# Two transformer blocks on one core: GpSimd's low parts, the first rows' products, the compressed scores and the rotations are ordered anew

## The chip, the cores and the metric

The kernel runs on one NeuronCore of a Trainium2 chip. Its engines run side by side, each in the order of its own instructions, and wait for each other by semaphores: TensorE (PE in the profile, its weight loads PEld) multiplies, VectorE (DVE), ScalarE (ACT) and GpSimd (POOL) work elementwise, and SyncE (SP) issues the loads of weights. SBUF is the memory on the chip; PSUM, with 8 banks, takes what TensorE writes. The metric is the time of one execution on the device in microseconds; lower is better.

## The reference, cut to what matters

A sequence of 256 tokens with 1024 features in float32 goes through two different blocks, each of two layers of three sublayers: a feed-forward, a token mixing, a feed-forward.

```python
# first block, per layer l
x = x + 0.5 * swiglu(rms_norm(x, ffn1_norm[l]), ffn1_wg[l], ffn1_wu[l], ffn1_wd[l])
z = rms_norm(x, mix_norm[l]) @ w_in[l]           # rq rk rv rg mq mk mv ca cg
rq, rk = rotary(to_heads(rq), ret_inv), rotary(to_heads(rk), ret_inv)
y_ret = silu(rg) * rms(retention(rq, rk, rv))    # scores * decay, times values
mq, mk = rotary(to_heads(mq), rope_inv), rotary(to_heads(mk), rope_inv)
y_moba = softmax(causal(mq @ mk.T / 8)) @ mv     # 256 tokens are one block
y_conv = conv_module(ca, cg, ...)                # 31 taps over the tokens
x = x + concat([y_ret, y_moba, y_conv]) @ w_out[l]
x = x + 0.5 * swiglu(rms_norm(x, ffn2_norm[l]), ...)
# second block, per layer: the same three steps, each with
n = rms_norm(h, norm_g[l, i]) * (1 + scale) + shift      # from cond @ ada_w
h = h + gate * sublayer(n)     # mixing: NSA with compressed scores, dilated, forgetting
```

## The kernel before

Every float32 product with weights is made of three passes: the weights `raw` are split into a high part `wh` (ScalarE, L2134) and a low part `wl` = raw - wh (VectorE, L2425), the activations into `xh` and `xl` (or `hTh`/`hTl`, `y1h`/`y1l`), and TensorE adds wh·xh, wl·xh and wh·xl (L1819, L1820, L1822). Weights come in units through 4 buffers `raw` and are split in pieces of two blocks of 128 rows ("subs") into 5 buffers each of `wh` and `wl`. Tokens are in two halves, t = 0 and 1, each with its own PSUM bank.

One class, `Order`, writes the order of all engines: its methods call hooks, and each engine's subclass issues its own instructions in them, so the program order of each engine is that of the calls. `take` and `ahead` split three to four pieces ahead of TensorE's use. `fill` first runs every posted function that is due (`post(f, lag)` makes it due `lag` pieces later; LAG is 3), then multiplies one piece of the current job and calls the job's `done`.

**Mixing of the first block** (`mix1`). The jobs are the column groups c, mq, mk, mv, rq, rk, rv, rg. `q_done` (for mq, mk, rq, rk) first gives VectorE three taps of the convolution (`taps(3)`, six instructions on `cacc`, L2637), then `heads_in`: ScalarE copies the rows into `zt` (L2261) and VectorE rotates them there (L2612 to L2617 over `rt`); a post turns `zt` on TensorE (L1792), and ScalarE copies it out (`Trq`, L2253). Beside the jobs runs `attention` over three groups of two heads: `scores` on TensorE (L1943), row minima on VectorE (L2569), exponentials on ScalarE (L2223), normalization (L2239), turns through banks 6 and 7 (L1792), `values` (L1969, always into bank 7), and then ScalarE's `y1h` (L2244) and VectorE's `y1l` (L2598), which frees bank 7. In a step, `values` stands after the first half's `fill`. Retention follows: `ret_scores` (L2015), `ret_decay` on VectorE (L2681, L2682), `ret_values` (L2024 to L2026, bank 7), which ScalarE empties (L2296), and `turn_wo`, which turns the result (`ym`) through a bank from `next_t`, which gives 6 and 7 in turn by `tbank`.

**Seams between sublayers of the second block** (`skewed`). There are six, at about 995, 1187, 1408, 1602, 1794 and 2015 us. The normalization's row scale (`ms` on VectorE L2465, `rr` on GpSimd L2837) becomes a diagonal matrix `dg` (VectorE, L2509), and TensorE turns and scales the input by it (L1866) for t = 0. `first_hi` multiplies t = 0 with what is there (L1880, L1883, L1887) while the other half is still being added up; then come the second diagonal, the second turn, and `first_lo` and `first_rest`. At all seams but the first, the two low parts that are still open go to GpSimd (`split_lo_pool`, L2831).

**Compressed scores** (`cmp_scores`, L2080, second block). Four heads, two rows of tokens each: 64-row products of 15 columns. Even heads lie in partitions 0 to 63 and write bank 4, odd heads in 64 to 127 and bank 5. Float32 products like these are two passes each in the profile.

Of the kernel before, what the change touches and what calls it, by code (L numbers as in the profile page):

```python
# [406 lines left out]
class Order:  # L407
# [120 lines left out]
    def lower(self, pool=False):  # L528

        j, u, k0, nk, w, last = self.later.pop(0)  # L530
        if pool:
            self.lo_at[j] = (self.s.plo, j)
            self.split_lo_pool(j, u, k0, nk, w)
        else:
            self.lo_at[j] = (self.s.lo, j)
            self.split_lo(j, u, k0, nk, w)
        if last:
            self.load(u + NR, self.lo_at[j], self.lo_at[j - 1] if k0 else None)
# [7 lines left out]
    def split_lo_pool(self, j, u, k0, nk, w):  # L546
        pass
# [263 lines left out]
    def skewed(self, label, banks):  # L811

        nx, add_1 = self.half
        s = nx[-1]
# [3 lines left out]
        two = nx[0] == "final"  # L818
# [16 lines left out]
        while self.later:  # L835
            self.lower(pool=not two)
# [388 lines left out]
    def heads_in(self, b, tk, zi, rot, rs):  # L1225
        z = self.m.zt[zi]
        for t in range(2):
            r = self.new(self.s.act, "zin")
            self.rows_part(z[:, t, 0:384], b[t], 384, tk, rs, t, ACT.Copy, self.zt_free[zi], r)
            self.free[b[t]] = r  # L1230
        if rot is not None:
            cos, sin, half, w = rot
            r = self.rotate(z[:, :, 0:384].rearrange("p t (n f) -> p t n f", f=64), cos, sin, 6, half, [r, w])
        return r

# [18 lines left out]
    def mix1(self, l, nx):  # L1254
# [31 lines left out]
        def q_done(n, zi, rot):  # L1286
            def done(b, tk):
                taps(3)
                r = self.heads_in(b, tk, zi, rot, True)

                def post():
                    rdy[n] = self.heads_out(m.qk[n], zi, r)
                self.post(post)
            return done
# [124 lines left out]
        ret_out(2)  # L1419
        turn_wo(0)  # L1420
# [364 lines left out]
class Tensor(Order):  # L1785
# [86 lines left out]
    def first_hi(self, js, b, x):  # L1872
# [11 lines left out]
        j, hs, nk, w = js[2]  # L1884
        self.wait_ge(self.lo_at[j])
        for n in range(nk):
            e.matmul(o, X[0](4 + n, 0), m.wl[hs][:, n * w:(n + 1) * w], start=False, stop=False)  # L1887
# [185 lines left out]
    def cmp_scores(self, l, qn):  # L2073
        m = self.m
        for h in (0, 2, 1, 3):
            lo, b = 64 * (h % 2), 4 + h % 2
            self.wait_ge((self.s.vec, ("kc", l)), *qn, self.free[b])
            for t in range(2):
# [742 lines left out]
class Pool(Order):  # L2821
# [4 lines left out]
    def split_lo_pool(self, j, u, k0, nk, w):  # L2826
# [3 lines left out]
        self.wait_ge((s.hi, j))  # L2830
# [188 lines left out]
```

## Time and profile before

| | us |
|---|---|
| median of 3 runs | 2216.21 (2215.99 to 2217.55) |
| profiled execution | 2214.64 |
| its span in the profile | 2212.8 |
| TensorE busy | 2188.6 (99%) |
| VectorE busy | 1536.3 (69%) |
| ScalarE busy | 1148.3 (52%) |
| GpSimd busy | 49.5 (2%) |
| chain that ended last | PE 91%, DVE 6%, ACT 1%, DMA 1% |

The granted TensorE clock is full throughout (0.999 in the mean). Busy time of TensorE contains the modelled ends of its pipelined passes, so what counts is from start to start: a pass of 512 columns starts every 0.23 us, one of 384 every 0.17 us. The rows of a timeline give the start in us from the beginning of the span, the time in us, the engine, the line of the code, the operation, what is written and read, the number of merged instructions, and in brackets the idle time before and what ended it.

### The profile page before, as it was taken

To read this page: it belongs to the slowest core of one execution; us is meant where nothing else is said; L and a number is where in the kernel's file an instruction comes from. 1 tells how busy PE (TensorE), PEld (TensorE's weight loads), DVE (VectorE), ACT (ScalarE), POOL (GpSimd) and SP (SyncE) were. 2 spreads that over 40 slices of the span, in tenths; PEclk is the share of its full clock that TensorE was granted. 3 is DMA by queue.
4 is the path that set the end of the run, shared out by engine and by line. 5 is a ranking of instruction groups with operands and counts; after the bars stand their busy time and mean duration, and the time that the engine had idled before them with its cause. 6 is when DMAs were issued, how large, how long until landed. Compare 5 with 4: busy or idle time off the path is not lost.

```text
span 2212.8 us, 27002 instructions
## 1 busy us (share of the span) xinstructions
PE 2188.6 (99%) x10836; PEld 1835.7 (83%) x10836; DVE 1536.3 (69%) x2339; ACT 1148.3 (52%) x1759; POOL 49.5 (2%) x42
## 2 busy tenths in 40 slices
PE   8999999999999999999999999999999999999998
PEld 6888888888888888888888977788888889778887
DVE  5655975557886978868785655788678756557664
ACT  5445654444445654445445655544454456555443
POOL 0000010000000010000001000100000010001000
PEclk9999999999999999999999999999999999999999
DMA  8554455556885557776776444577767864445653
GB/s 294 195 193 152 157 172 174 187 202 229 284 283 160 163 191 266 261 263 221 274 276 190 138 150 152 189 267 276 256 228 278 283 196 140 142 152 176 233 200 124
DMA packets 250641, 462.93 MB, mean 209 GB/s; under 512 B 9798, under 2 KB 55792, under 8 KB 250388
## 3 DMA queue, kind: packets, MB, share of 16 engines
q1 hardware_dynamic: 250276, 461.05, 61.0%
q8 instruction: 85, 1.39, 0.2%
q14 instruction: 40, 0.33, 0.0%
q10 hardware_dynamic: 240, 0.16, 0.0%
HBM read 460.12 MB, written 1.05 MB: 208 GB/s over the span
## 4 chain that ended last, share of the span: by engine, by line
PE 91%; DVE 6%; ACT 1%; DMA 1%; issue 0%; POOL 0%; SPq 0%; POOLq 0%; DVEq 0%; ACTq 0%
PE ps L1819 18%; PE ps L1822 18%; PE ps L1820 18%; PE s L1822 8%; PE s L1819 8%; PE s L1820 8%; PE ps L1792 3%; DVE wl L2425 2%; DVE cacc L2637 1%; PE s L1943 1%; PE ps L1835 1%; PE ps L1833 1%; PE ps L1834 1%; PE ps L1969 1%; DVE gts L2811 1%; PE ps L1866 1%
## 5 line engine op out<-in xcount | busy, mean ns | idle before, releaser
L2425 DVE TENSOR_TENSOR wl<-raw,wh 128x1024 fp32r<-128x1024 f32 (+1 forms) x734 | 853.2, 1179 | 218.2 <-ACT wh L2134 213.9
L2134 ACT ACTIVATE wh<-raw 128x1024 fp32r<-128x1024 f32 (+2 forms) x744 | 750.2, 1027 | 463.8 <-PE ps L1822 254.1
L1819 PE MATMUL ps<-wh,xh 128*128 128x512 f32 (+3 forms) x1632 | 619.9, 380 | 1.7 <-DVE wl L2425 1.7
L1822 PE MATMUL ps<-wh,xl 128*128 128x512 f32 (+3 forms) x1632 | 609.9, 374 | 0.0
L1820 PE MATMUL ps<-wl,xh 128*128 128x512 f32 (+3 forms) x1632 | 609.6, 374 | 0.0
L1819 PEld LDWEIGHTS ps<-wh,xh 128*128 128x128 f32 x1632 | 306.6, 188 | 57.0 <-issue 9.5
L1822 PEld LDWEIGHTS ps<-wh,xl 128*128 128x128 f32 x1632 | 306.5, 188 | 47.0
L1820 PEld LDWEIGHTS ps<-wl,xh 128*128 128x128 f32 x1632 | 306.8, 188 | 44.9
L2433 DVE SCALAR_TENSOR_TENSOR acc<-raw,condT,acc 128x512 f32<-128x512 f32 x252 | 188.6, 748 | 5.1
L1819 PE MATMUL s<-wh,xh 128*128 128x512 f32 x384 | 150.3, 391 | 0.0
L1822 PE MATMUL s<-wh,xl 128*128 128x512 f32 x384 | 149.6, 390 | 0.0
L1820 PE MATMUL s<-wl,xh 128*128 128x512 f32 x384 | 149.5, 389 | 0.0
L1819 PE MATMUL s<-wh,hTh 128*128 128x512 f32 x352 | 138.5, 394 | 0.0
L1822 PE MATMUL s<-wh,hTl 128*128 128x512 f32 x352 | 137.3, 390 | 0.0
L1820 PE MATMUL s<-wl,hTh 128*128 128x512 f32 x352 | 137.1, 390 | 0.0
L2216 ACT ACTIVATE hTh<-ps 128x512 fp32r<-128x512 f32 x88 | 48.3, 596 | 162.3 <-PE ps L1792 162.3
L2561 DVE TENSOR_TENSOR hTl<-ps,hTh 128x512 fp32r<-128x512 f32 x88 | 57.0, 686 | 104.0 <-ACT hTh L2216 103.9
L1819 PE MATMUL ps<-wh,hTh 128*128 128x512 f32 x268 | 104.6, 390 | 0.0
L1822 PE MATMUL ps<-wh,hTl 128*128 128x512 f32 x268 | 104.3, 389 | 0.0
L1820 PE MATMUL ps<-wl,hTh 128*128 128x512 f32 x268 | 104.3, 389 | 0.0
L1822 PEld LDWEIGHTS s<-wh,xl 128*128 128x128 f32 x384 | 72.1, 188 | 15.1
L1819 PEld LDWEIGHTS s<-wh,xh 128*128 128x128 f32 x384 | 72.1, 188 | 14.9
(357 smaller groups left out, 2471.3 us busy)
## 6 DMA issues: line engine op xcount, KB each, us to landing
raw<-in_ffn_w_in SPq DMA_DIRECT2D x80, 1024.0 KB, 5.2
raw<-in_ada_w SPq DMA_DIRECT2D x72, 1024.0 KB, 6.0
raw<-in_ffn_wg SPq DMA_DIRECT2D x40, 1024.0 KB, 5.2
raw<-in_ffn_wu SPq DMA_DIRECT2D x40, 1024.0 KB, 5.2
raw<-in_ffn_wd SPq DMA_DIRECT2D x40, 1024.0 KB, 5.3
raw<-in_ffn_w_out SPq DMA_DIRECT2D x40, 1024.0 KB, 6.4
raw<-in_mix_w_in SPq DMA_DIRECT2D x28, 1024.0 KB, 5.1
raw<-in_w_in SPq DMA_DIRECT2D x28, 768.0 KB, 4.3
```

Of the source, the lines that this page charges most:

```text
L1792: return self.e.transpose(out, src, self.m.ident[0:n, 0:n])
L1819: e.matmul(o, X[0](kk, t), hi, start=kk == 0, stop=False)
L1820: e.matmul(o, X[0](kk, t), lo, start=False, stop=False)
L1822: ins = e.matmul(o, X[1](kk, t), hi, start=False, stop=kk == K - 1)
L1833: e.matmul(o, X[0](kk, t), hi, start=kk == 0, stop=False)
L1834: e.matmul(o, X[0](kk, t), lo, start=False, stop=False)
L1835: ins = e.matmul(o, X[1](kk, t), hi, start=False, stop=kk == K - 1)
L2134: ins = self.e.activation(m.wh[j % NH][:, 0:n], m.raw[u % NR][:, k0 * w:k0 * w + n], ACT.Copy)
L2216: self.then_inc(self.e.activation(m.hTh[:, k:k + 2, :].rearrange("p k s -> p (k s)"), m.ps[b], ACT.Copy), th)
L2425: ins = self.e.tensor_tensor(m.wl[j % NH][:, 0:n], m.raw[u % NR][:, k0 * w:k0 * w + n], hi, ALU.subtract)
L2433: ins = self.e.scalar_tensor_tensor(out=a, in0=m.raw[u % NR][:, k * 512:k * 512 + 512], scalar=m.condT[:, kk:kk + 1], in1=a if kk else m.b ...
L2561: self.then_inc(self.e.tensor_tensor(lo, m.ps[b], hi.bitcast(F32), ALU.subtract), tl)
```

## The change

GpSimd's low parts wait, beside their high part, for the first diagonal (`("dg", s, 0)`). In `first_hi` the two low products of the third piece come before the high products of the fourth. `cmp_scores` goes over the heads inside of the loop over the rows of tokens. `heads_in` is cut in two, and `q_done` of the first block's mixing posts taps and rotation for the next `fill`. `tbank` is set to 7 ahead of `turn_wo(0)`, so that this turn takes bank 6.

```diff
-    def lower(self, pool=False):
+    def lower(self, pool=None):
...
-            self.split_lo_pool(j, u, k0, nk, w)
+            self.split_lo_pool(j, u, k0, nk, w, pool)
...
         while self.later:
-            self.lower(pool=not two)
+            self.lower(pool=None if two else (self.s.vec, ("dg", s, 0)))
...
+    def heads_rows(self, b, tk, zi, rs):
+        z = self.m.zt[zi]
         for t in range(2):
             r = self.new(self.s.act, "zin")
             self.rows_part(z[:, t, 0:384], b[t], 384, tk, rs, t, ACT.Copy, self.zt_free[zi], r)
             self.free[b[t]] = r
         return r
+
+    def heads_turn(self, zi, rot, r):
+        cos, sin, half, w = rot
+        z = self.m.zt[zi][:, :, 0:384].rearrange("p t (n f) -> p t n f", f=64)
+        return self.rotate(z, cos, sin, 6, half, [r, w])
...
             def done(b, tk):
-                taps(3)
-                r = self.heads_in(b, tk, zi, rot, True)
+                r = self.heads_rows(b, tk, zi, True)
+
+                def turn():
+                    taps(3)
+                    self.heads_turn(zi, rot, r)
 
                 def post():
-                    rdy[n] = self.heads_out(m.qk[n], zi, r)
+                    rdy[n] = self.heads_out(m.qk[n], zi, self.rt_free)
+                self.post(turn, 0)
                 self.post(post)
...
         ret_out(2)
+        self.tbank = 7
         turn_wo(0)
...
-        j, hs, nk, w = js[2]
-        self.wait_ge(self.lo_at[j])
-        for n in range(nk):
-            e.matmul(o, X[0](4 + n, 0), m.wl[hs][:, n * w:(n + 1) * w], start=False, stop=False)
+            if i == 2:
+                self.wait_ge(self.lo_at[j])
+                for n in range(nk):
+                    e.matmul(o, X[0](4 + n, 0), m.wl[hs][:, n * w:(n + 1) * w], start=False, stop=False)
...
-        for h in (0, 2, 1, 3):
-            lo, b = 64 * (h % 2), 4 + h % 2
-            self.wait_ge((self.s.vec, ("kc", l)), *qn, self.free[b])
-            for t in range(2):
+        self.wait_ge((self.s.vec, ("kc", l)), *qn, self.free[4], self.free[5])
+        for t in range(2):
+            for h in range(4):
+                lo, b = 64 * (h % 2), 4 + h % 2
...
-        self.wait_ge((s.hi, j))
+        self.wait_ge((s.hi, j), after)
```

VectorE in the first mixing, from the last piece ahead of the rotation of `rq` to the next piece (wl_NN and wh_NN are the five buffers, raw_NN the four, `cacc` the taps, zt_105 the rows of `rq`, `y1l` the first group's low part). Before:

```order
L2425 TENSOR_TENSOR wl_65<-raw_54,wh_60 128x768 [waits s_hi]
L2637 SCALAR_TENSOR_TENSOR cacc<-upad,cols_68,cacc 128x256 [waits s_vec] x6
L2612 TENSOR_TENSOR rt_134<-zt_105,cos_72 128x384 [waits s_act]
L2613 TENSOR_TENSOR rt_135<-zt_105,sin_73 128x384
L2614 TENSOR_TENSOR rt_136<-zt_105,cos_72 128x384
L2615 TENSOR_TENSOR rt_137<-zt_105,sin_73 128x384
L2616 TENSOR_TENSOR zt_105<-rt_134,rt_135 128x2x6x32 [waits s_vec]
L2617 TENSOR_TENSOR zt_105<-rt_136,rt_137 128x2x6x32
L2598 TENSOR_TENSOR y1l<-ps,y1h 128x256 [waits s_act]
L2425 TENSOR_TENSOR wl_66<-raw_54,wh_61 128x768
```

The same place now (the lines of the code are 11 higher):

```order
L2436 TENSOR_TENSOR wl_65<-raw_54,wh_60 128x768 [waits s_hi]
L2609 TENSOR_TENSOR y1l<-ps,y1h 128x256 [waits s_act]
L2648 SCALAR_TENSOR_TENSOR cacc<-upad,cols_68,cacc 128x256 [waits s_vec] x6
L2623 TENSOR_TENSOR rt_134<-zt_105,cos_72 128x384
L2624 TENSOR_TENSOR rt_135<-zt_105,sin_73 128x384
L2625 TENSOR_TENSOR rt_136<-zt_105,cos_72 128x384
L2626 TENSOR_TENSOR rt_137<-zt_105,sin_73 128x384
L2627 TENSOR_TENSOR zt_105<-rt_134,rt_135 128x2x6x32 [waits s_vec]
L2628 TENSOR_TENSOR zt_105<-rt_136,rt_137 128x2x6x32
L2436 TENSOR_TENSOR wl_66<-raw_54,wh_61 128x768
```

`y1l`, which waits for ScalarE, moved from behind six taps and the rotation to ahead of them; the place of `rk` a group later, and both in the second layer, moved in the same way. At `mq` and `mk`, where no group is under way, the rotation moved behind two more taps. ScalarE's and SyncE's orders are the same as before.

TensorE at the second seam, from the third piece's high products to the second turn (`dg` the diagonal, s and ps PSUM banks). Before:

```order
L1880 MATMUL ps<-wh_59,xh 128x512 [waits s_act]
L1880 MATMUL ps<-wh_59,xh 128x512
L1880 MATMUL ps<-wh_60,xh 128x512 [waits s_act]
L1880 MATMUL ps<-wh_60,xh 128x512
L1887 MATMUL ps<-wl_64,xh 128x512 [waits s_plo]
L1887 MATMUL ps<-wl_64,xh 128x512
L1866 MATMUL s<-dg,x 128x128 [waits s_vec]
```

And now:

```order
L1891 MATMUL ps<-wh_59,xh 128x512 [waits s_act]
L1891 MATMUL ps<-wh_59,xh 128x512
L1898 MATMUL ps<-wl_64,xh 128x512 [waits s_plo]
L1898 MATMUL ps<-wl_64,xh 128x512
L1891 MATMUL ps<-wh_60,xh 128x512 [waits s_act]
L1891 MATMUL ps<-wh_60,xh 128x512
L1877 MATMUL s<-dg,x 128x128 [waits s_vec]
```

The two low products moved ahead of the wait for the fourth piece's activations, at all six seams; what stands behind them is still the turn by the second diagonal.

## Rows read from the trace of the kernel before

**Rows 1.** The page, busy time of TensorE: us, share of the span, instructions.
```profile
PE 2188.6 (99%) x10836; PEld 1835.7 (83%) x10836; DVE 1536.3 (69%) x2339; ACT 1148.3 (52%) x1759; POOL 49.5 (2%) x42
```

**Rows 2.** Waits of PE: total us, how many times, the longest.
```profile
PE ps L1866 <- DVE dg L2509: 3.0, 2, 2.7
...
PE ps L1880 <- ACT xh L2200: 1.6, 6, 0.5
...
PE ps L1792 <- ACT ptT L2229: 1.1, 2, 0.5
```

**Rows 3.** Busy us of each engine (instructions), clock, DMA, first block's mixing.
```profile
237.00:273.00 36.00, 35.00 (x220) 31.05 (x219) 35.63 (x94) 25.80 (x65) 0.00 (x0) 1.00 0.49 152
```

**Rows 4.** Timeline of DVE: start, us, line, op, out<-in, count, idle before.
```profile
248.79 2.46 DVE L2637 SCALAR_TENSOR_TENSOR cacc<-upad,cols,cacc 128x256 f32<-128x256 f32 x6
...
254.44 0.95 DVE L2425 TENSOR_TENSOR wl<-raw,wh 128x768 fp32r<-128x768 f32 x1
...
257.76 0.28 DVE L2569 CUSTOM_DVE_ANT_0 pt<-s,cst 128x128 f32<-128x128 f32 x1
```

**Rows 5.** Timeline of ACT in the same stretch.
```profile
251.53 0.37 ACT L2244 ACTIVATE y1h<-ps 128x256 fp32r<-128x256 f32 x1
...
258.08 0.40 ACT L2223 ACTIVATE pt<-pt,small 128x128 f32<-128x128 f32 x1 [2.37 <-DVE small L2569]
...
260.59 0.84 ACT L2253 ACTIVATE Trq<-ps 128x512 f32<-128x512 f32 x2
```

**Rows 6.** Timeline of PE, same stretch and some 14 us on.
```profile
258.18 0.82 PE L1792 MATMUL ps<-cst,zt 128*128 128x128 f32 x6
...
261.49 0.76 PE L1969 MATMUL ps<-ptT,mv 128*64 128x256 f32 x6 [0.38 <-ACT Trq L2253]
...
275.15 0.92 PE L2015 MATMUL s<-Trq,Trk 64*128 64x256 f32 x8
```

**Rows 7.** Timeline of DVE, the next group and the first decay.
```profile
261.71 2.46 DVE L2637 SCALAR_TENSOR_TENSOR cacc<-upad,cols,cacc 128x256 f32<-128x256 f32 x6
...
267.36 0.95 DVE L2425 TENSOR_TENSOR wl<-raw,wh 128x768 fp32r<-128x768 f32 x1
...
273.86 0.42 DVE L2681 TENSOR_TENSOR pt<-s,cst 128x256 f32<-128x256 f32 x1 [0.57 <-PE s L2015]
```

**Rows 8.** Timeline of ACT, the next group's high part.
```profile
264.38 0.38 ACT L2244 ACTIVATE y1h<-ps 128x256 fp32r<-128x256 f32 x1
```

**Rows 9.** Timeline of DVE, first op of the rotation of `mq`.
```profile
220.76 0.26 DVE L2612 TENSOR_TENSOR rt<-zt,cos 128x96 f32<-128x96 f32 x1 [0.56 <-ACT zt L2261]
```

**Rows 10.** Timelines of DVE, POOL and PE at the seam at 1408.
```profile
1408.52 2.35 DVE L2509 TENSOR_SCALAR dg<-cst,rr 128x128 f32<-128x128 f32 x1 [0.66 <-POOL rr L2837]
...
1408.45 4.66 POOL L2831 TENSOR_TENSOR wl<-raw,wh 128x1024 fp32r<-128x1024 f32 x2
...
1411.02 0.68 PE L1866 MATMUL ps<-dg,x 128*128 128x128 f32 x4 [2.74 <-DVE dg L2509]
```

**Rows 11.** Timelines of DVE and PE, second diagonal at the seam at 1602.
```profile
1608.26 0.29 DVE L2509 TENSOR_SCALAR dg<-cst,rr 128x128 f32<-128x128 f32 x1 [0.44 <-POOL rr L2837]
...
1608.71 0.56 PE L1866 MATMUL s<-dg,x 128*128 128x128 f32 x3
```

**Rows 12.** Timelines of POOL and DVE at the seam at 2015.
```profile
2015.45 4.76 POOL L2831 TENSOR_TENSOR wl<-raw,wh 128x1024 fp32r<-128x1024 f32 x2
...
2019.95 0.27 DVE L2465 SCALAR_TENSOR_TENSOR ms<-ssq 128x1 f32<-128x1 f32 x1
```

**Rows 13.** Timeline of PE at the seam between the blocks.
```profile
1000.44 0.73 PE L1880 MATMUL ps<-wh,xh 128*128 128x512 f32 x2 [0.49 <-ACT xh L2200]
```

**Rows 14.** Timeline of PE: compressed scores, then a group's scores.
```profile
1229.56 1.53 PE L2080 MATMUL s<-small,qn 64*128 64x15 f32 x16
...
1242.13 0.93 PE L1943 MATMUL s<-kd,qn 64*128 64x128 f32 x8
```

**Rows 15.** Timeline of PE, turn of the retention's output.
```profile
295.67 0.41 PE L1792 MATMUL ps<-cst,ym 128*128 128x128 f32 x2 [0.57 <-ACT zt L2296]
```

More of the change, by code:

```diff
@@ L544, in split_lo, with split_lo_pool @@
         pass
-    def split_lo_pool(self, j, u, k0, nk, w):
+    def split_lo_pool(self, j, u, k0, nk, w, after):
         pass
@@ L1223, in rotate_part @@
         pass
-    def heads_in(self, b, tk, zi, rot, rs):
+    def heads_rows(self, b, tk, zi, rs):
         z = self.m.zt[zi]
@@ L1230, in heads_in @@
             self.free[b[t]] = r
-        if rot is not None:
-            cos, sin, half, w = rot
-            r = self.rotate(z[:, :, 0:384].rearrange("p t (n f) -> p t n f", f=64), cos, sin, 6, half, [r, w])
-        return r
+        return r
+    def heads_turn(self, zi, rot, r):
+        cos, sin, half, w = rot
+        z = self.m.zt[zi][:, :, 0:384].rearrange("p t (n f) -> p t n f", f=64)
+        return self.rotate(z, cos, sin, 6, half, [r, w])
+    def heads_in(self, b, tk, zi, rot, rs):
+        r = self.heads_rows(b, tk, zi, rs)
+        return r if rot is None else self.heads_turn(zi, rot, r)
     def heads_out(self, dst, zi, after, scale=1.0):
@@ L2824, with split_lo_pool @@
     engine = "POOL"
-    def split_lo_pool(self, j, u, k0, nk, w):
+    def split_lo_pool(self, j, u, k0, nk, w, after):
         m, s = self.m, self.s
```

## The prediction

> **What bounds the kernel now.** I read the page's busy times first: TensorE is busy for 2188.6 us of the 2212.8 us span [rows 1]. So an edit gains only where TensorE stands still or where it streams fewer or better overlapped passes, and it loses wherever it makes TensorE wait. The waits by engine then give what can be won: 3.0 us behind the diagonals, 1.6 us in six places behind the high parts `xh`, and pieces of about 0.5 us in the two mixing sublayers of the first block [rows 2]. Last I read where another engine is about to become the bound. In the stretch in which the first block's mixing scores, turns and rotates, VectorE is busy for 35.63 us of 36.00, with TensorE at 35.00 beside it [rows 3]. There VectorE has no slack, and whatever makes it stand still comes back as a TensorE wait.
>
> **Part 1, the rotations later.** This is the largest term. In the order, the low part of an attention group's values (`y1l`) has moved ahead of six taps and the rotation of `rq`, and after that of `rk`. VectorE runs in order, and `y1l` waits for ScalarE's high part `y1h`. Before the change VectorE ended a `wl` piece at 248.79, ran taps and rotation, and went on with the next `wl` at 254.44, with `y1l` in between and no wait [rows 4]. `y1h` ended at 251.53 + 0.37 = 251.90 [rows 5]; its place on ScalarE and what is ahead of it there are not changed. So VectorE would now reach `y1l` at 248.79 and stand still until 251.93. Behind it is the same work as before, 254.44 - 248.79 = 5.65, so the next `wl` starts at 257.58 instead of 254.44: 3.14 us late, with six taps, the rotation, a `wl` and the next group's row minima queued behind the wait.
>
> Who waits for that: the row minima at 257.76 [rows 4] come at 260.90. ScalarE had waited 2.37 us for them at 258.08, and its copy of the turned `rq`, which frees PSUM bank 7, ends at 260.59 + 0.84 = 261.43 [rows 5]. TensorE's products with the values need that bank and had already waited 0.38 us for it at 261.49 [rows 6]. They move to 264.63. The turns of `rq` at 258.18 [rows 6] still find the rotation ended, about 257.7.
>
> The second time goes the same way. VectorE was free at 261.71, now at 264.85; `y1h` ends at 264.38 + 0.38 = 264.76, shifted by the same 3.14 to 267.90 [rows 7, 8]. VectorE stands still for another 3.05 us, and the `wl` of 267.36 [rows 7] starts at 267.93 + 5.65 = 273.58, 6.22 late. The next op that TensorE needs is the retention decay at 273.86, before which VectorE had been idle for 0.57 us [rows 7]; it is 6.22 - 0.57 = 5.65 late, and so are the scores of the second pair of heads at 275.15, which need the banks that the decays free [rows 6]. Nothing later gives that back, since TensorE is the engine that sets the end. What is gained inside: the rotation of `mq` no longer waits 0.56 us for ScalarE, as two more taps stand ahead of it [rows 9]. It bounds the gain at 0 and 0.56; I take 0.3, since later scores wait for TensorE and not for VectorE. That is **5.3 us lost in each of the two mixing sublayers, 10.6 us**. Its bounds are 0 per sublayer (if the backlog is absorbed, rival 1) and 6.2 (if the 0.57 us are not).
>
> **Part 2, GpSimd behind the first diagonal.** At 1408 GpSimd started its two low parts at 1408.45 and VectorE's diagonal, started at 1408.52, took 2.35 us; TensorE waited 2.74 us and started 0.15 us after its end [rows 10]. At 1608 the same op took 0.29 us [rows 11]. With the wait the diagonal is never held: 2.35 - 0.29 = 2.06 us gained, at this one of five places. The wait has a price. At 2015 GpSimd started at 2015.45 for 4.76 us, and VectorE's sum `ms`, ready at 2019.95, took 0.27 us, until GpSimd was done at 2020.21 [rows 12]. GpSimd would now start after the diagonal, 0.25 us later there, and `ms`, the row scale, the second diagonal and TensorE's second turn follow by as much. At 1408 I take 0.3 and for the other three 0.1 together, since there GpSimd just ends before `ms`. **Sum: 2.06 - 0.3 - 0.25 - 0.1 = 1.4 us gained.** The rows show a diagonal and a sum that end only with GpSimd's op. The Trainium skill, SBUF — State Buffer, section "SBUF: two separate sides", says that the port pair of VectorE and GpSimd is an exclusive lock which whichever engine starts first keeps for the whole instruction. By that rule, the trace agrees with both numbers, 2.35 and 0.27 us; without it the later start would cost nothing and the part would give 2.0 us.
>
> **Part 3, the first rows' products reordered.** Two low products now fill the place where TensorE waits for the last `xh`: at most 0.49 us at 1000.44 [rows 13] and about 0.22 us in each of the five others. In those five it gains nothing. The second diagonal starts at 1608.26 for 0.29 us, and TensorE's second turn starts at 1608.71, which is its end plus the 0.15 us of rows 10 [rows 11]. TensorE would only arrive early and wait there. At 1000.44 the row scale isn't the bound, so I take 0.45, between 0 and 0.49. **0.45 us gained.**
>
> **Part 4, the compressed scores.** Sixteen passes of 15 columns take 1.53 us with each head's two rows of tokens behind each other, while eight passes of 128 and 256 columns, whose heads alternate between the two halves of the array, take 0.93 [rows 14]. If alternation overlaps the short ones in pairs as well, a half, 0.77, is the most that can go; nothing is the least. I take 0.4, since the four long pairs show about 0.2 us a pair, and eight short ones at half that come to 0.8 with a tail of 0.3. Two sublayers: **0.8 us gained.** The Trainium skill, TensorEngine Tiling (Array Packing), section "Theoretical Speedup", gives up to 2 times for a contraction of 64 or less. By that the part would be an estimated 1.5 us instead of 0.8.
>
> **Part 5, the bank of the retention's turn.** TensorE waited 0.57 us at 295.67 for ScalarE to empty bank 7, just written by the last retention values [rows 15]. The turn now takes bank 6. Between 0 and 0.57; I take 0.4, since `y1h` and `y1l` of that turn must be ready half a piece of weights later. Twice: **0.8 us gained.** The other mixing sublayers and feed-forwards get banks 6 and 7 swapped; the first block's two mixings ran alike, so I put that at nothing.
>
> **Sum.** Gains 1.4 + 0.45 + 0.8 + 0.8 = 3.45; loss 10.6; together 7.1 us slower. The profiled execution was 2214.64 us with a span of 2212.8, and the median of three is 2216.21; the sum of changes is put on the median: 2223.3 us (the profiled one would be 2221.8).
>
> **The rivals.** (1) The backlog is absorbed: VectorE catches up before TensorE needs anything, so part 1 costs between 0 and 3.8 us per sublayer. For it: after 273 VectorE has room, and pieces of `wl` are made three to four pieces ahead. Against it: the 2.37 us that ScalarE waited on VectorE and the bank that TensorE waited on already [rows 5, 6]. It gives -3.4 to +4.2 us, 2212.8 to 2220.4. (2) On the other side, faster: `y1h` comes early enough, so `y1l` first only frees bank 7 sooner. TensorE's turns of the next group then lose their waits, 1.1 us in two places that the profile puts on ScalarE's `ptT` [rows 2]; my reading is that they wait for `y1l`, which frees the same bank. It decides at `y1h` ending before 248.8 instead of 251.9, and gives -3.45 - 1.1 - 0.8 (short gaps of the same kind) = -5.4, 2210.8. Against it stands that `y1h` sits behind four normalizations in ScalarE's unchanged order. (3) The wait for the diagonal turns against itself, GpSimd's low part being late for TensorE: its first op ends 2.4 us after its start, with more than a us in hand, so I give it no place of its own. The change does in the order what it says.
>
> **How the numbers follow.** The forecast, 2223.3, has a chance of 0.68 and by itself the range 2220.7 to 2226.5 (part 1 between 4 and 6.2 per sublayer, parts 2 to 5 at their ends). Rival 1 has 0.20, rival 2 has 0.12. About 0.2% of the time, 4.4 us, is what a measurement of this kernel can tell from no change. So slower 0.68, within 0.2% 0.20, faster 0.12. The range is 2213.0 to 2226.5: it holds rival 1 and leaves out rival 2 and a few in a hundred above.
>
> **What would show each step.** Part 1: VectorE idle for about 3 us before `y1l` twice in each first-block mixing, waits of TensorE of 3 us more before the values' products, and 5 us more from the first scores to the first retention values. Part 2: every diagonal at 0.29 us, none behind GpSimd, and second diagonals up to 0.3 us later against the first. Part 3: no wait on `xh`, and a new one on the second diagonal in five places. Part 4: sixteen passes in about 1.1 us. Part 5: no wait of the kind of rows 15. I am wrong if VectorE isn't idle at `y1l`, or if it is and TensorE's row is no later at the first retention values.

## The result, and the profile after

The changed kernel takes 2225.12 us (median of 6 executions, 2223.75 to 2226.77), the kernel before 2217.1 us beside it (median of 6, 2215.99 to 2218.05). The ratio is 1.0038, with a 95% interval of 1.0028 to 1.0048: some 8 us, or 0.4%, slower. The profiled execution of after took 2226.47 us with a span of 2224.4. One execution of the kernel before, at 2921 us, is left out of all ratios and counts.

The waits of TensorE in after (engine, tile and line that waited, what for, us in all, times, longest us). The line numbers of the code are 11 higher than in the kernel before:

```profile
PE ps L1980 <- ACT Trq L2264: 7.1, 2, 3.7
PE ps L1803 <- DVE y1l L2609: 2.4, 1, 2.4
PE s L1877 <- DVE dg L2520: 2.4, 5, 0.7
...
PE ps L1877 <- DVE dg L2520: 1.0, 2, 0.7
```

Against [rows 2] the first two are new and long: the values' products wait 3.7 us for `Trq`, and once, for 2.4 us, some transposes wait for `y1l`. The 3.0 us for `dg` have become 1.0, the six waits on `xh` are gone, and five waits on the second diagonal are new. Now VectorE in the first mixing (start, us, engine, line, operation, in brackets the idle time and who ended it):

```profile
253.23 0.42 DVE L2609 TENSOR_TENSOR y1l<-ps,y1h 128x256 fp32r<-128x256 f32 x1 [3.06 <-ACT y1h L2255]
...
269.22 0.42 DVE L2609 TENSOR_TENSOR y1l<-ps,y1h 128x256 fp32r<-128x256 f32 x1 [2.99 <-ACT y1h L2255]
...
280.72 0.42 DVE L2692 TENSOR_TENSOR pt<-s,cst 128x256 f32<-128x256 f32 x1
```

The two idle stretches before `y1l` are as long as worked out. The decays at 280.72 stood at 273.86 [rows 7] and have no idle time before them. TensorE in the first mixing and then in the second:

```profile
265.93 1.33 PE L1980 MATMUL ps<-ptT,mv 128*64 128x256 f32 x6 [3.66 <-ACT Trq L2264]
...
281.11 0.66 PE L1803 MATMUL ps<-cst,cacc 128*128 128x128 f32 x4
282.01 0.92 PE L2026 MATMUL s<-Trq,Trk 64*128 64x256 f32 x8 [0.24 <-DVE pt L2693]
...
762.52 0.87 PE L1980 MATMUL ps<-ptT,mv 128*64 128x256 f32 x8 [3.42 <-ACT Trq L2264]
...
779.21 0.63 PE L1803 MATMUL ps<-cst,cacc 128*128 128x128 f32 x4 [2.44 <-DVE y1l L2609]
```

The transposes of the convolution's output `cacc` go straight on in the first mixing (281.11) and wait 2.44 us in the second (779.21). The kernel before had no wait in either. Two things were not in the prediction: this wait, and the speed of the passes behind the waits. Busy time of the engines by stretch of after (stretch, its length, then PE, PEld, DVE, ACT, POOL busy with their counts, the granted TensorE clock, DMA share, GB/s):

```profile
266.00:272.00 6.00, 6.00 (x22) 5.29 (x23) 3.01 (x9) 4.27 (x10) 0.00 (x0) 0.50 0.47 150
272.00:284.00 12.00, 11.76 (x81) 10.63 (x81) 11.19 (x26) 6.70 (x12) 0.00 (x0) 1.00 0.52 171
...
780.50:784.20 3.70, 3.70 (x16) 3.59 (x13) 3.40 (x9) 0.91 (x1) 0.00 (x0) 0.54 0.18 50
```

Behind the wait of 3.66 us TensorE was granted 0.50, its level of 1.2 GHz, and made 22 passes in 6 us; afterwards it was back at 1.00, 2.4 GHz. In [rows 3] the clock was 1.00 all through.

**Where the time went.** For each matmul the start after less the start before gives an offset. The table has the change of that offset over each part, for the profiled executions; the columns beside it are kernels of the next section.

| part (us in the trace of before) | forecast | after | part 1 taken back | best version |
| --- | --- | --- | --- | --- |
| start of the program (up to 18) | 0 | +1.7 | +2.0 | +1.4 |
| first mixing (225 to 290) | +5.3 | +5.21 | +0.05 | -0.37 |
| retention's turn (290 to 305) | -0.4 | -0.41 | -0.45 | -0.45 |
| second mixing (725 to 783) | +5.3 | +7.57 | +1.04 | -0.43 |
| retention's turn (783 to 800) | -0.4 | -0.44 | -0.44 | -0.45 |
| `acl` (925 to 950) | 0 | +0.35 | -0.56 | -0.09 |
| first rows' products at 1000 | -0.45 | -0.40 | -0.41 | -0.44 |
| compressed scores, both | -0.8 | -0.94 | -0.94 | -0.94 |
| seam at 1408 | -1.76 | -1.71 | -1.69 | -1.69 |
| four other seams | +0.35 | +0.47 | +0.50 | +0.49 |
| last matmul | +7.1 | +11.5 | -0.8 | -3.1 |

Small drifts between the rows make up the rest. The 11.5 us of the traces are more than the 8 us of the medians, since the two profiled executions stand at opposite ends: 2214.64 us is below the before's median and 2226.47 above the after's. The first row, 1.7 us, goes with no part of the change. Passes of 512 columns started every 0.43 us instead of 0.23 between 12 and 16 us. This came in 7 of the 13 traces of changed kernels; after has it, and the kernel `taps_first` of the next section, which holds all five parts too, has not. How many of the executions behind the medians have it isn't known.

The seam at 1408, where the first diagonal had taken 2.35 us [rows 10], in after: TensorE, then VectorE, then GpSimd.

```profile
1422.18 0.68 PE L1877 MATMUL ps<-dg,x 128*128 128x128 f32 x4 [0.66 <-DVE dg L2520]
...
1428.13 1.13 PE L1877 MATMUL s<-dg,x 128*128 128x128 f32 x8 [0.68 <-DVE dg L2520]
```

```profile
1421.75 0.29 DVE L2520 TENSOR_SCALAR dg<-cst,rr 128x128 f32<-128x128 f32 x1 [0.66 <-POOL rr L2848]
...
1426.36 0.56 DVE L2476 SCALAR_TENSOR_TENSOR ms<-ssq 128x1 f32<-128x1 f32 x1 [0.15 <-ACT junk L2165]
...
1427.69 0.29 DVE L2520 TENSOR_SCALAR dg<-cst,rr 128x128 f32<-128x128 f32 x1 [0.44 <-POOL rr L2848]
```

```profile
1422.18 4.73 POOL L2842 TENSOR_TENSOR wl<-raw,wh 128x1024 fp32r<-128x1024 f32 x2 [0.47 <-DVE dg L2520]
1427.00 0.66 POOL L2848 TENSOR_TENSOR rr<-ms,cst 128x1 f32<-128x1 f32 x1
```

The diagonal takes 0.29 us. The price is as read: `ms` lasts 0.56 us instead of 0.16, until GpSimd's op ends at 1426.91, the row scale `rr` follows at 1427.00, and TensorE's second turn waits 0.68 us for the second diagonal.

The compressed scores, [rows 14] before:

```profile
1243.25 1.07 PE L2091 MATMUL s<-small,qn 64*128 64x15 f32 x16
```

1.07 us for the sixteen passes instead of 1.53.

### The profile page after: what moved, and what is told of

It reads as the page before. It is cut to its first block, busy times and chain, and to the rows that moved or that the text cites. A ratio compares the mean times of both kernels' runs of the same rounds, so it can differ in the third digit from the quotient of the medians.

```text
span 2224.4 us, 27009 instructions
## 1 busy us (share of the span) xinstructions
PE 2194.9 (99%) x10836; PEld 1843.0 (83%) x10836; DVE 1535.7 (69%) x2339; ACT 1148.1 (52%) x1759; POOL 48.6 (2%) x42
## 4 chain that ended last, share of the span: by engine, by line
PE 92%; DVE 5%; ACT 2%; DMA 1%; issue 0%; POOL 0%; ACTq 0%; POOLq 0%; SPq 0%; DVEq 0%
PE ps L1830 19%; PE ps L1833 18%; PE ps L1831 18%; PE s L1830 8%; PE s L1833 8%; PE s L1831 8%; PE ps L1803 4%; PE s L1954 1%; DVE wl L2436 1%; PE ps L1846 1%; PE ps L1844 1%; PE ps L1845 1%; DVE cacc L2648 1%; PE ps L1980 1%; DVE gts L2822 1%; PE ps L1877 1%
```

## The experiments

Twelve kernels, each timed beside the kernel before on the same chip. The main theory: part 1 costs some 5.2 us in each first-block mixing by making VectorE stand still; the swapped banks, which the prediction put at nothing, cost the rest of the second mixing; and the half clock behind TensorE's long waits may or may not add to either. The rivals are named with each run.

### Part 1 taken back

```diff
             def done(b, tk):
-                r = self.heads_rows(b, tk, zi, True)
-                def turn():
-                    taps(3)
-                    self.heads_turn(zi, rot, r)
+                taps(3)
+                r = self.heads_in(b, tk, zi, rot, True)
...
-                self.post(turn, 0)
                 self.post(post)
```

> The changed kernel with part 1 taken back: taps and rotation stand again where they stood before, parts 2 to 5 stay. Theory, by the offsets between the two traces: part 1 is the only part that costs much, 5.6 us in the first mixing and up to 8.1 in the second. Without it no wait of VectorE of 3 us before y1l, no 3.7 us wait of TensorE before the values' products, granted clock 1.0 there. What stays: -1.2 us at the five seams (-1.7 at 1408, +0.1 to +0.3 at the others), -0.4 at 1000, -0.5 at each set of compressed scores, -0.4 twice at the retention's turn, and a cost of about 1.1 in the second mixing, where the swapped banks make the transposes of cacc (before at 766.67) wait for y1l (ended at 767.20 + 0.42). Sum -2.3 us, 2214.8. Rival: the swapped banks cost nothing by themselves, sum -3.4, 2213.7. Rival: the loss is not in part 1 (the other edits or the slow clock cause it), time stays above 2221.

Measured: 2213.45 us, before 2216.02, ratio 0.9983 (0.9974 to 0.9992). Both mixings are back, but the second keeps 1.04 us (table above). The sum of the trace without its first row is -2.8, and the rival that the loss lies elsewhere falls. The time is nearer to the 2213.7 of the rival in which the swap costs nothing than to 2214.8, but the trace shows the 1.04 us and the wait on `y1l`. Waits of TensorE:

```profile
PE s L1873 <- DVE dg L2516: 2.4, 5, 0.7
PE ps L1799 <- DVE y1l L2605: 1.8, 2, 1.0
```

### Part 1 alone

The edit above, the other way, in the kernel before.

> The kernel before with part 1 alone. Theory: VectorE idle for 3.1 us before two y1l in each first-block mixing, 5.3 to 5.6 us lost in each, so +10.6 to +11.2, 2227.7 to 2228.3, and both mixings alike since no bank is swapped; the transposes of cacc do not wait in either. The granted clock falls to half behind the wait of 3.7 us before the values' products, hidden behind VectorE's own lateness. Rival: the second mixing costs 8.1 as in the changed kernel, because the lateness alone makes the transposes of cacc wait, +13.5, 2230.6. Rival (backlog absorbed): under +4.

Measured: 2227.36 us, before 2216.02, ratio 1.0048 (1.0034 to 1.0061), some 11 us. By the trace +5.16 in the first mixing and +5.12 in the second. So without swapped banks the two are alike, and lateness alone does not make the transposes of `cacc` wait for `y1l`. They waited 0.20 us, for `cacc` itself:

```profile
777.26 0.63 PE L1802 MATMUL ps<-cst,cacc 128*128 128x128 f32 x4 [0.20 <-DVE cacc L2647]
```

### The retention's turn in bank 6, alone

```diff
         ret_out(2)
+        self.tbank = 7
         turn_wo(0)
```

> The kernel before with part 5 alone (the retention's turn takes bank 6). Theory: 0.4 us gained at each of the two turns; the banks are swapped from there on, so in the second mixing the transposes of cacc share a bank with the y1l whose subtraction ended at 767.62 and cannot start at 766.67: 1.0 to 1.1 us lost at that place, a wait of TensorE on y1l, none in the first mixing. Sum +0.3, 2217.4. Rival: the swap costs only when VectorE is late, no wait at cacc, sum -0.8, 2216.3.

Measured: 2217.08 us, before 2216.02, ratio 1.0003 (0.9994 to 1.0012). The time can't tell the two apart, the trace can: -0.45 at each turn, +1.03 in the second mixing, and this wait of TensorE, right behind VectorE's `y1l`:

```profile
767.03 0.63 PE L1793 MATMUL ps<-cst,cacc 128*128 128x128 f32 x4 [1.03 <-DVE y1l L2599]
```

```profile
766.46 0.42 DVE L2599 TENSOR_TENSOR y1l<-ps,y1h 128x256 fp32r<-128x256 f32 x1
```

The values always go to bank 7, the turns alternate between 6 and 7. Setting the alternation by hand at one place moved every turn behind it to the other bank, and so the transposes of `cacc` of the second mixing to bank 7, just filled by the values. The part was worth nothing in its first form: two gains of 0.45 against one loss of 1.03.

This trace showed more. Behind the first diagonal at 1408, which is held by GpSimd here as before, TensorE ran at half clock, which the kernel before did not do in its profiled execution; the offset grew by 2.34 us there:

```profile
1410.40:1416.50 6.10, 6.07 (x22) 5.57 (x23) 2.61 (x8) 2.94 (x8) 2.11 (x1) 0.50 0.48 146
```

### The changed kernel with the banks' turn put back

```diff
-        self.tbank = 7
+        tb, self.tbank = self.tbank, 7
         turn_wo(0)
+        self.tbank = 13 - tb
```

> The changed kernel, with the banks' turn put back after the first product of part 5, so that the second mixing has the same banks as the first. Theory: the 2.44 us wait of the cacc transposes at 779.21 and the half-clock stretch behind it go; the second mixing costs 5.6 us like the first, not 8.1; 2.4 to 4.0 us below the changed kernel, 2221.1 to 2222.7. Rival: the wait comes from VectorE's lateness and stays, 2225.1.

Measured: 2223.14 us, ratio 1.0030 (1.0019 to 1.0041). Second mixing +5.12, first +5.19, both turns still -0.43. The 2.44 us wait is gone, and the next scores wait for the decays in its place:

```profile
776.19 0.63 PE L1804 MATMUL ps<-cst,cacc 128*128 128x128 f32 x4 [0.20 <-DVE cacc L2649]
778.12 0.92 PE L2027 MATMUL s<-Trq,Trk 64*128 64x256 f32 x8 [1.30 <-DVE pt L2694]
```

So the swap cost 7.57 - 5.12 = 2.45 us in the changed kernel and 1.03 where VectorE is in time. The wait itself is not the larger share of the 2.45. By the offsets, the changed kernel lost 2.47 us from 763 us of the trace of before to these scores and the kernel with the banks put back 1.57, for it waits at the decays instead: 0.9 us between them. Behind the scores the changed kernel lost another 1.55 us, in the stretch at half clock (780.50 above), and the other one nothing. The transposes wait 2.44 us because `y1l` stands behind the late decays, and the clock falls behind that wait.

### Part 1 for rq alone, and for rk alone

```diff
-            return done
+            return later if n in ("rq",) else now
```

`later` is the new form, `now` the old one; `("rk",)` in the second kernel.

> The kernel before with part 1 for rq alone (mq, mk and rk as before). Theory A (VectorE's lateness alone decides, as in the prediction's sum): one idle stretch of 3.14 us per mixing, less the 0.57 us that VectorE had in hand before the decays: 2.6 us per mixing, +5.2, 2221.2; TensorE's half-clock stretch is hidden. Theory B (the clock decides where VectorE is less late): TensorE still waits 3.7 us before the values' products, runs for some 6 us at half clock behind it, and by that is 6 us late itself at the next turns, as the changed kernel showed at 267 us (7.28 - 1.30 against before); so 5 to 5.4 us per mixing although VectorE's part is only 2.6; +10 to +11, 2226 to 2227.

> The kernel before with part 1 for rk alone. Theory: one idle stretch of 3.05 us of VectorE per mixing, at the second y1l; no wait at the values' products of 261.49 beyond the 0.38 there was, decays 3.05 - 0.57 = 2.5 us late, TensorE waits 2.5 us for them before the second pair's scores: +2.5 per mixing, +5.0, 2221.0. If the granted clock falls behind that wait as well, 1 to 2 us more per mixing, up to +9. Rival: VectorE makes it up by the decays, under +1.

Measured: `rq` alone 2225.71 us, before 2216.44, ratio 1.0041 (1.0026 to 1.0057), by the trace +5.22 and +3.93 in the two mixings. `rk` alone 2221.27, ratio 1.0022 (1.0012 to 1.0031), +2.45 and +2.37. The parts add up to 7.67 in the first mixing, both together cost 5.16. Theory B holds for `rq` in the first mixing: by VectorE's account 2.6 us were lost, TensorE lost 5.2. In the second it lost 3.93, between A's 2.6 and B's 5 to 5.4; the clock was at 0.78 over the 6 us there and at 0.50 in the first. With `rk` alone TensorE's waits are short and the clock stays at 1.00. Of `rq` alone first TensorE's row, then the stretches:

```profile
266.76 1.55 PE L1987 MATMUL ps<-ptT,mv 128*64 128x256 f32 x8 [3.69 <-ACT Trq L2271]
```

```profile
266.00:272.00 6.00, 5.24 (x20) 4.53 (x21) 5.97 (x14) 4.75 (x11) 0.00 (x0) 0.50 0.55 179
...
761.00:767.00 6.00, 3.17 (x15) 2.69 (x16) 5.92 (x16) 6.00 (x18) 0.00 (x0) 0.78 0.58 196
```

and of `rk` alone the first mixing's stretch and the waits of TensorE:

```profile
266.00:272.00 6.00, 4.90 (x31) 4.32 (x31) 5.97 (x13) 2.56 (x7) 0.00 (x0) 1.00 0.00 0
```

```profile
PE s L2033 <- DVE pt L2700: 2.6, 2, 1.3
PE ps L1810 <- DVE zt L2635: 2.2, 2, 1.1
```

Each mixing has 1.1 us for the turned `rk` and 1.3 for the decays, 2.4 in all.

### The wait filled with transposes

```diff
         o, fresh = m.ps[7], group.compressed is None
+        self.nvalue = getattr(self, "nvalue", 0) + 1
+        if self.nvalue in FILLED:       # FILLED = (2, 5)
+            self.wait_ge(self.free[4])
+            for i in range(22):
+                self.transpose(m.ps[4][:, 0:P], m.x[:, 0, 0:P])
         self.wait_ge(self.free[7])
```

Once in the kernel with part 1 alone, and once in the one with `rq` alone.

> The kernel before with part 1, and in each first-block mixing 22 transposes of x (0.109 us each, 2.4 us, into a score bank that is overwritten later) in the place where TensorE waits 3.7 us before the values' products. They fill the wait but add none, since they end before the bank is free. Theory: the half clock behind that wait comes from the standing still; with it filled the granted clock stays 1.0 in the 6 us behind it. The time changes little against part 1 alone (2227.4), because VectorE, 5.6 us late at the decays, decides there anyway: 2226.5 to 2227.5. Rival: the half clock is part of the loss, time falls by 2 to 6 us. Rival: the clock falls all the same (it has another cause).

> The kernel before with part 1 for rq alone, and the 22 transposes of x in the place where TensorE waits before the values' products. With rq alone and nothing in the wait each mixing cost 5.4 and 4.1 us: 3.3 of wait, 2.6 and 1.5 of half clock, less 0.7 that a later wait gave back. Theory: with the wait filled the clock stays 1.0, the half clock's share goes and 2.6 us per mixing is left, +5.2 in all, 2221.6 against 2225.7 for the same kernel without the transposes. Rival: the half clock was hidden here too (VectorE decides), time stays at 2225 to 2226.

Measured with the whole of part 1: 2226.37 us, ratio 1.0047 (1.0034 to 1.0061), so no less than without them (1.0048); +5.19 and +5.13 in the mixings. With `rq` alone: 2223.63 us, before 2217.08, ratio 1.0027 (1.0017 to 1.0037) against 1.0041; +3.21 and +3.17 instead of +5.22 and +3.93. The place in the kernel with `rq` alone, then its stretches:

```profile
263.25 2.62 PE L1811 MATMUL s<-cst,x 128*128 128x128 f32 x22 [0.63 <-DVE small L2593]
...
266.28 0.87 PE L1993 MATMUL ps<-ptT,mv 128*64 128x256 f32 x8 [0.41 <-ACT Trq L2277]
```

```profile
266.00:272.00 6.00, 5.56 (x35) 4.98 (x35) 5.97 (x14) 5.14 (x12) 0.00 (x0) 1.00 0.52 167
...
761.00:767.00 6.00, 5.59 (x37) 4.98 (x35) 5.96 (x14) 5.33 (x12) 0.00 (x0) 1.00 0.56 178
```

With two waits of 0.63 and 0.41 us in place of one of 3.69, the clock stays at 1.00 and the products with the values still start as soon as `Trq` is there. In both kernels the clock fell because TensorE stood still. Whether that costs anything depends on who is late behind it. With `rq` alone it cost 2.0 and 0.8 us. The 3.2 us that are left are the wait itself (0.63 and 0.41, and the 2.62 of the transposes, less the 0.38 of before). I had expected 2.6, VectorE's 3.14 less its 0.57 in hand. But TensorE loses the time at the values already, and what VectorE has in hand at the decays doesn't give it back. With `rq` and `rk` it cost nothing: VectorE's second idle stretch makes the decays 5.2 us late, and TensorE, full clock or half, can't pass them.

### The six taps ahead of y1l again

```diff
             def done(b, tk):
+                taps(3)
                 r = self.heads_rows(b, tk, zi, True)
                 def turn():
-                    taps(3)
                     self.heads_turn(zi, rot, r)
```

> The changed kernel with the six taps put back ahead of the values' subtraction; only the rotation itself stays behind y1l. Theory (the lateness is the time that VectorE stands still for y1h, and six taps of 0.40 us fill 2.4 of the 3.1): VectorE stands still for about 0.7 us before each of the two y1l, the decays are 1.4 - 0.57 = 0.8 us late, TensorE's wait before the values' products is about 1.1 us and the granted clock stays 1.0. Against the kernel before: 2 x 0.8, less 0.6 twice for the earlier first chain, plus the bank wait of 1.0, less what the other parts gave, 3.4: about -2, 2214.5. Rival: the place of the rotation matters and not the taps (the rotation behind y1l makes rk's turn late): 2219 or more.

Measured: 2215.84 us, before 2217.08, ratio 0.9994 (0.9985 to 1.0004). VectorE's idle time before `y1l` in the first mixing:

```profile
251.64 0.42 DVE L2609 TENSOR_TENSOR y1l<-ps,y1h 128x256 fp32r<-128x256 f32 x1 [0.69 <-ACT y1h L2255]
...
265.27 0.42 DVE L2609 TENSOR_TENSOR y1l<-ps,y1h 128x256 fp32r<-128x256 f32 x1 [0.61 <-ACT y1h L2255]
```

As worked out, 0.7 us each, and the first mixing costs +0.45 instead of +5.21. The second costs +2.85, where I had 0.8 - 0.6 + 1.0 = 1.2. The transposes of `cacc` waited longer than the 1.03 us, and the clock fell behind that wait too. First TensorE, then the stretch:

```profile
767.90 0.63 PE L1803 MATMUL ps<-cst,cacc 128*128 128x128 f32 x4 [1.92 <-DVE y1l L2609]
```

```profile
769.00:775.00 6.00, 6.00 (x36) 5.69 (x33) 4.87 (x10) 1.52 (x4) 0.00 (x0) 0.75 0.38 127
```

By the offsets the passes behind the wait lost 1.55 us more, as in the changed kernel. So a wait of 1.92 us was enough for a fall here, while waits of 2.72 to 2.74 us at 1408 left the clock at 1.00 in three traces. The rival, 2219 or more by the place of the rotation alone, falls.

### GpSimd behind the first diagonal, alone, and parts 3 and 4, alone

```diff
-            self.lower(pool=not two)
+            self.lower(pool=None if two else (self.s.vec, ("dg", s, 0)))
...
-        self.wait_ge((s.hi, j))
+        self.wait_ge((s.hi, j), after)
```

The second kernel has the new order in `first_hi` and in `cmp_scores`.

> The kernel before with part 2 alone. Theory from the offsets of the kernels that hold it: -2.06 at 1410, +0.4 at the second diagonal behind it, +0.3 at 2020, nothing at 1000, 1208, 1608 and 1800: -1.35 in the trace. In two of six traces in which the diagonal was held, TensorE ran at half clock behind that wait of 2.74 us, which cost 1.4 us more (one 2.3); that goes too, so the median may fall by 1.4 to 3 us: 2213.4 to 2215. Rival: GpSimd's later start costs at each seam what it saved, 2216.4.

> The kernel before with parts 3 and 4 alone (the first rows' products, the compressed scores). Theory: -0.45 at 1000, nothing at the five seams of the later blocks, where the second diagonal decides and a new wait on it of 0.2 to 0.3 us takes the place of the one on xh, -0.48 at each set of compressed scores: -1.4, 2215.0. Rival: the five seams gain 0.2 us each as well, -2.4, 2214.0.

Measured: part 2 alone 2213.72 us, before 2217.08, ratio 0.9986 (0.9978 to 0.9995), some 3 us; by the trace -1.69 at 1408, +0.06, +0.09, +0.07 and +0.26 at the others, -1.2 in all. Parts 3 and 4 alone 2213.77 us, ratio 0.9987 (0.9978 to 0.9997); by the trace -0.41 at 1000, -0.47 at each set of compressed scores, and at most 0.02 at the four later seams other than 1408. The five seams did not gain the 0.2 us each of the rival. The waits of TensorE show why:

```profile
PE ps L1866 <- DVE dg L2509: 3.0, 2, 2.7
PE s L1866 <- DVE dg L2509: 1.5, 5, 0.4
PE ps L1845 <- DVE acl L2440: 1.5, 1, 1.5
```

The second line is the new wait on the second diagonal, in five places, where `xh` had been waited for. The interval of this kernel (0.7 to 4.9 us less) holds the 1.35 us of the trace but doesn't decide between the two theories.

The diagonal of 1408 is held in eight of the traces of this study, the kernel before's among them. In five of them the clock fell behind it. Of the kernel before, and then of the one with parts 3 and 4 alone, the 6 us from TensorE's start:

```profile
1411.00:1417.00 6.00, 5.77 (x34) 4.71 (x35) 3.63 (x11) 4.38 (x12) 2.77 (x2) 1.00 0.44 149
```

```profile
1411.10:1417.10 6.00, 6.00 (x27) 5.55 (x28) 2.63 (x8) 3.01 (x9) 2.07 (x1) 0.72 0.45 140
```

The offset grew by 1.0 to 2.3 us in the five, 1.0 on average over the eight. In the six kernels with part 2 the wait is 0.66 us and the clock never fell there. The executions without a trace agree. Their mean granted clock is on record: 0.998 in 59 of 74 executions of the kernel before and 0.999 in the other 15, of which kind the profiled one is; 0.999 or more in all 33 of part 2 alone, of part 1 taken back and of the best version. The 59 took 0.8 to 1.4 us longer in the mean than the 15, by the chip. So some 0.9 us of the gain of part 2 alone is the half clock that no longer comes. This estimate and the trace's 1.2 make 2.1 us; the median's 3 lies above, inside an interval of 1.1 to 4.9, and what is left between the two isn't shown. The place of the fall in these executions is inferred from the traces, where no kernel without a long wait in the mixings fell anywhere but at 1408 before TensorE's last pass.

### The parts that gain, together

The changed kernel, with the rotations of `rq` and `rk` back in their place (`later if n in ("mq", "mk") else now`) and the banks' turn put back.

> The changed kernel with the rotations of rq and rk taken back to their place (those of mq and mk stay later) and with the banks' turn put back after the first product of part 5. By the offsets measured so far: -0.4 twice for the earlier chain in front of the first probabilities, -0.45 twice at the retention's turn, -0.45 at 1000, -0.5 twice at the compressed scores, -1.65 at 1408 and +0.3 at 2020, no bank wait: sum -4.4 against the kernel before, 2211.6; against the changed kernel without part 1 (2213.45) -1.8. Rival: the 1.03 us bank wait was only moved elsewhere, or mq and mk later cost as rq and rk do: 2213.5 or more.

Measured: 2210.76 us, before 2216.44, ratio 0.9973 (0.9964 to 0.9982), and 0.9935 of the changed kernel, by one ratio over the other. By the trace it stands 4.5 us ahead of the kernel before, leaving out its slow first passes; the medians are 5.7 apart, with the half clock at 1408 in most executions of the kernel before. Both mixings now gain 0.4 us. Waits of TensorE:

```profile
PE s L1886 <- DVE dg L2529: 2.4, 5, 0.7
...
PE ps L1989 <- ACT Trq L2273: 0.8, 2, 0.4
PE ps L1812 <- ACT ptT L2249: 0.5, 1, 0.5
PE ps L1812 <- DVE y1l L2618: 0.5, 1, 0.5
```

Next in line is the second diagonal, 2.4 us in five places: 1.5 of it is there with parts 3 and 4 alone, the rest comes with GpSimd's later start, which holds `ms` and with it `rr`.

## Why the prediction was right, and where it was not

**Part 1** was right in place, mechanism and size, and stands by three experiments: undone, alone, and with the taps back. Forecast 5.3 us per mixing, measured 5.2; forecast idle stretches 3.14 and 3.05, measured 3.06 and 2.99; the values' products 3.14 later, measured 4.44 - 1.30 = 3.14, where 1.30 is the offset just ahead of the first group's `y1l`. The gain of 0.3 inside it, the rotation of `mq` no longer waiting, is 0.38 in the trace. Two points were missing. The bank that `y1l` frees sooner, which the prediction had only in rival 2, does give 0.20 us per mixing at the probabilities' turn (254.67 in the trace of before, where the offset goes from 1.30 to 1.10 in after and from 1.43 to 1.23 with part 1 alone). And the sum of VectorE's terms was not the only path to 5.2: TensorE, at half clock behind its 3.7 us wait, is as late by itself. For an edit of `rq` alone the sum would have been short by 2.6 us in the first mixing and by 1.3 in the second.

**Part 5** has the step that failed: "The other mixing sublayers and feed-forwards get banks 6 and 7 swapped; the first block's two mixings ran alike, so I put that at nothing." The two ran alike because both had the same banks, so that they were no sample of the other order. With the swap, one set of transposes falls on the bank that the values have just filled: 1.03 us by itself; 2.45 us with VectorE late, 0.9 by the longer wait and 1.5 by the half clock behind it; all in the second mixing. The gain at the two turns was 0.41 and 0.44, against 0.4 forecast.

**Part 2**: 2.06 at the diagonal, 0.39 given back behind it against 0.3, 0.28 at 2015 against 0.25, 0.19 in the other three against 0.1; 1.2 us against 1.4. The price read in the rows is there: `ms` lasts 0.56 us at 1426.36, and 0.57 at the seam of 2015. What was not seen is that the wait of 2.74 us is in some executions followed by a stretch at half clock.

**Part 3** gained 0.40 at 1000 (forecast 0.45) and nothing elsewhere, and the new wait on the second diagonal is in the five places named. **Part 4** gained 0.46 and 0.47 (forecast 0.4 each). The Trainium skill, TensorEngine Tiling (Array Packing), section "Theoretical Speedup", gives up to 2 times, which would have made an estimated 0.77 us of the 1.53; with 1.07 the sixteen short passes did not reach it.

**The time.** Forecast +7.1, measured +8.0 with an interval of 6.2 to 10.6. By the trace, without the first passes, it is +9.8: the 2.4 of the banks, most of it half clock, is the one large term that the sum lacked, 0.35 at `acl` and the 0.2 of part 2 are small ones. Against that the kernel before loses some 1.0 us on average at 1408 by the half clock, which the traced execution didn't show and which after doesn't have. So part of the agreement of 2223.3 with 2225.1 comes from two omissions of opposite sign. Rival 1 falls, since nothing was absorbed in either mixing. Rival 2 falls as a whole, and its mechanism is worth 0.4 us.

**What stays open.** At `acl` (925 to 950) the offset moved by -0.56 to +1.21 us in the thirteen kernels, in both directions and with no part in common; no run tells the cause. Why the first passes are slow in seven of the thirteen traces is open as well; what they are is not. Of after:

```profile
12.00:16.00 4.00, 3.93 (x9) 3.15 (x10) 4.00 (x8) 3.91 (x9) 0.00 (x0) 1.00 1.05 388
```

Nine passes in 4 us are those of the lower level; the kernel before made 16 there. The 1.00 of this row isn't a measurement. The trace's records of the clock begin at 16.11 us here, with the full level, and a stretch without a record is shown as 1.00. The passes change from 0.43 to 0.23 us apart at that same time, at 16.07. In all seven traces with slow first passes the records begin at 15.4 to 16.8 us, in the other seven, the kernel before's among them, at 10.0 to 11.8, before the first pass of 512 columns.

## What to carry to other kernels

On an engine that has no slack, moving a step that waits for another engine ahead of steps that don't costs nearly the whole wait, each time (VectorE stood still for 6.05 us in a mixing, and TensorE lost 5.2), and it can be read from two end times before anything is run. Where buffers alternate, an edit that sets the alternation by hand moves every later user, so it has to be put back, or each later user has to be looked at against who filled that buffer before. Two sublayers that run alike in the profile say nothing on an order that neither of them had.

## What the runs showed of the hardware

A wait of TensorE can cost more than its length. After 3.4 to 3.7 us of standing still the granted clock fell to its lower level all eight times (four kernels, two mixings each), for some 4 to 6 us of work; after 2.72 to 2.74 us in five of eight traces; after 2.44 and after 1.92 us in the one trace each that has such a wait. After 1.73 us, the longest below these (in the trace of before, at 12.24), and less it never fell. Filling the wait with 22 transposes kept it at 1.00 all four times. The same kernel does both: in 59 of 74 executions of the kernel before the mean granted clock was 0.998, in 15 it was 0.999. The Trainium skill, TensorE: Matmul & The Clock Gate, section "Part 1: The HAM clock gate (the "warmup" mystery)", says that the point of a change of level differs from run to run of one kernel; these executions agree.

What the fall costs depends on who is late behind it: 2.0 and 0.8 us with `rq` alone, 1.55 us twice behind the waits of 2.44 and 1.92, 1.0 to 2.3 us at 1408, where TensorE sets the end; nothing where another engine is later still. Two late chains side by side cost the longer one: in the first mixing 5.2 us with both rotations moved, 2.4 with `rk` alone, and 5.2 or 3.2 with `rq` alone, with and without the fall.

In the kernel before GpSimd started its first op at 1408.45 and ended it at 1410.79; VectorE's diagonal, 0.29 us elsewhere, started at 1408.52 and ended at 1410.87. In after, the sum `ms`, a single column (0.16 us elsewhere), took 0.56 us and ended at 1426.92, GpSimd's second op at 1426.91. This fits the exclusive lock on the port pair of VectorE and GpSimd in the Trainium skill, SBUF — State Buffer, section "SBUF: two separate sides", which the prediction named beside the 0.65 us that it took off part 2; measured were 0.86. The page has the lock for VectorE's ops in a two-port mode or with two inputs in SBUF, and no run here shows which of these two ops is such. Moving GpSimd behind the one op put it in front of the other.
